# The first norm's row factor moved behind the projection, and the first weight unit in two halves

## The reference, cut to what matters

```
x: (256 tokens, 1024)
h = x * rsqrt(mean(x*x, per token) + 1e-6) * norm1_g
t = h @ w_in                                # 1792 + 1048 + 2048 columns
aq, ak, bq, bks, bkw | av, bvs, bvw, bkc, bvc, bgate | mgate = columns of t
kc, vc = MLP over windows of bkc, bvc;  ya, yb = two kinds of attention
g = sigmoid(mgate + b_merge)                # (256, 2, 1024)
x = x + (g[:,0] * (ya @ w_up_a) + g[:,1] * (yb @ w_up_b)) @ w_out
x = x + peer_ffn(...)                       # then cross-attention, FFNs
```

## Time and profile before

| | us |
|---|---|
| runs shown: median (lowest, highest) | 1786.71 (1786.55, 1787.03) |
| the profiled execution | 1786.81 |
| its span, from the first to the last instruction | 1785.0 |
| TensorE busy | 1750.7 |
| VectorE, ScalarE, GpSimd busy | 1204.4, 1001.4, 489.2 |

### The profile page before, as it was taken

One profiled execution on the slowest core, in us unless ns is written; L12 is line 12 of the kernel. 1 busy time (PEld: TensorE's weight loads), 2 busy tenths in 40 slices (PEclk: granted clock), 3 DMA queues, 4 the chain that ended last, 5 costly groups with the idle time before them and its releaser, 6 DMA issues.

```text
span 1785.0 us, 30696 instructions
## 1 busy us (share of the span) xinstructions
PE 1750.7 (98%) x10764; PEld 1545.4 (87%) x10764; DVE 1204.4 (67%) x2466; ACT 1001.4 (56%) x1679; POOL 489.2 (27%) x245
## 2 busy tenths in 40 slices
PE   8998999999999999999999999999999999999998
PEld 7895899899878888888888888877999988989997
DVE  6757849899765555555555555876579965669974
ACT  5567565469445555555555555666565545556553
POOL 0150166379144444444444444000000000000000
PEclk9999999999999999999999999999999999999999
DMA  7560454601455555555556665634455564545552
GB/s 292 200 236 13 150 193 152 226 25 48 165 194 193 189 189 191 192 191 188 188 190 237 239 216 177 241 142 166 145 192 189 189 199 144 177 131 177 189 196 76
DMA packets 84719, 313.70 MB, mean 176 GB/s; under 512 B 9360, under 2 KB 9488, under 8 KB 83216
## 3 DMA queue, kind: packets, MB, share of 16 engines
q1 hardware_dynamic: 82912, 304.44, 50.8%
q10 hardware_dynamic: 1712, 7.97, 1.2%
HBM read 304.77 MB, written 7.60 MB: 175 GB/s over the span
## 4 chain that ended last, share of the span: by engine, by line
PE 85%; issue 6%; DVE 4%; ACT 3%; POOL 2%; PEld 1%; DMA 0%; DVEq 0%; POOLq 0%; ACTq 0%; PEldq 0%
PE bank L798 80%; PE bank L1249 3%; POOL wsplit L1400 1%; ACT projq L1579 1%; ACT probs L1579 0%; POOL wsplit L1431 0%; PEld bank L1249 0%; PE bank L843 0%; PE bank L832 0%; DVE wsplit L1891 0%; DVE projq L2106 0%; DVE att L2092 0%; DVE attn L2089 0%; PE bank L1070 0%; DVE probs L2104 0%
## 5 line engine op out<-in xcount | busy, mean ns | idle before, releaser
L798 PE MATMUL bank<-HT,wsplit 128*128 128x256 f32 (+1 forms) x5056 | 720.3, 301 | 1.6 <-DVE HT L1934 0.9
L798 PEld LDWEIGHTS bank<-HT,wsplit 128*128 128x128 f32 x5056 | 679.1, 189 | 47.4 <-issue 3.7
L1431 POOL TENSOR_TENSOR wsplit<-raw,wsplit 128x1024 fp32r<-128x1024 f32 x111 | 278.0, 2505 | 380.1 <-ACT wsplit L1757 380.1
L798 PE MATMUL bank<-wsplit,wexp 128*128 128x512 f32 x1536 | 371.0, 392 | 0.6 <-DVE wexp L2372 0.6
L1757 ACT ACTIVATE wsplit<-raw 128x1024 fp32r<-128x1024 f32 x238 | 240.2, 1053 | 181.0 <-PE bank L798 180.6
L798 PEld LDWEIGHTS bank<-wsplit,wexp 128*128 128x128 f32 x1536 | 280.2, 188 | 57.1 <-DVE wsplit L2347 2.1
L2347 DVE TENSOR_TENSOR wsplit<-raw,wsplit 128x1024 fp32r<-128x1024 f32 x127 | 156.9, 1236 | 103.8 <-ACT wsplit L1757 103.6
L1466 ACT ACTIVATE wsplit<-raw 128x1024 fp32r<-128x1024 f32 x148 | 156.4, 1059 | 111.6 <-PE bank L798 110.5
L1891 DVE TENSOR_TENSOR wsplit<-raw,wsplit 128x1024 fp32r<-128x1024 f32 x124 | 154.5, 1258 | 78.5 <-ACT wsplit L1466 77.6
L1891 DVE TENSOR_TENSOR wsplit<-raw1b,wsplit 128x1024 fp32r<-128x1024 f32 x102 | 122.5, 1221 | 44.0 <-ACT wsplit L1466 43.6
L1466 ACT ACTIVATE wsplit<-raw1b 128x1024 fp32r<-128x1024 f32 x102 | 107.5, 1058 | 76.3 <-PE bank L798 72.0
(11 more groups left out here) (288 smaller groups left out, 2070.2 us busy)
## 6 DMA issues: line engine op xcount, KB each, us to landing
raw<-weights SPq DMA_DIRECT2D x148, 512.0 KB, 4.2
raw<-expert_v SPq DMA_DIRECT2D x127, 512.0 KB, 3.8
raw<-expert_u SPq DMA_DIRECT2D x119, 512.0 KB, 4.3
raw1b<-weights SPq DMA_DIRECT2D x102, 512.0 KB, 4.3
raw1a<-weights SPq DMA_DIRECT2D x48, 512.0 KB, 4.5
early_u<-expert_u SPq DMA_DIRECT2D x5, 512.0 KB, 3.7
raw1a<-expert_u SPq DMA_DIRECT2D x4, 512.0 KB, 4.3
parked<-memT SPq DMA_DIRECT2D x1, 2048.0 KB, 7.3
```

The costliest lines, as they stand in the source:

```text
L798: ins = pe.matmul(out, lhsT, rhs, start=start, stop=stop, **kw)
L1431: pool.tensor_tensor(wsplit[:, s, 1, :], raw0[:, s, :], f32(wsplit[:, s, 0, :]), ALU.subtract).then_inc(u_lo, 1)
```

## The change

TensorE transposes X unscaled, the first group of columns as soon as each token block has landed, with no filling before and five filling products behind. The squares, roots and reciprocals come later on ScalarE and VectorE. Where the projection has tokens on the partitions, its copies out of the banks multiply by the factor. For the merge gates the factors have to run along the free dimension: VectorE spreads each block's factors over 128 columns of `act_e`, TensorE transposes them behind the projection, ScalarE copies the result into `row_of_tokens`. VectorE multiplies a gate's bank by that row into `mgate` and frees the bank; ScalarE's sigmoid then works in `mgate`. Gate 7's copy becomes such a product on VectorE. The first weight unit is loaded, rounded and split in two halves, and TensorE begins with its first.

```diff
@@ -101,11 +101,11 @@ def bank_groups()
-    out += [(("mg", 0), "a")] + [(("win2", kv), "d") for kv in range(2)]
-    out += [(("mg", g), "a") for g in range(1, 4)]
-    out += [(("hid", kv), "d") for kv in range(2)] + [(("mg", 4), "a")]
+    out += [(("mg", 0), "d")] + [(("win2", kv), "d") for kv in range(2)]
+    out += [(("mg", g), "d") for g in range(1, 4)]
+    out += [(("hid", kv), "d") for kv in range(2)] + [(("mg", 4), "d")]
...
@@ -329,6 +329,7 @@
+        row_of_tokens, row_factors = act_e[:, 0, :], act_e[:, 1, :]
@@ -675,7 +678,9 @@ SyncE
-            for u in range(4):
+            sp.dma_start(raw0[:, 0, 0:512], weights[0][:, 0:512]).then_inc(first_landed, 16)
+            sp.dma_start(raw0[:, 0, 512:1024], weights[0][:, 512:1024]).then_inc(w_landed[0], 16)
+            for u in range(1, 4):
                 load(u, u)
@@ -879,12 +884,27 @@ TensorE
+            def first_unit(banks, src, fresh):
+                for k in range(2):
+                    if k == 0:
+                        pe.wait_ge(first_lo, 1)
+                        w = lambda part: wsplit[:, 0, part, :].rearrange("p (k n) -> p k n", k=2)
+                    else:
+                        w = tiles_of(weights_of("win", 0, 0), k=2)
+                    wait_turned(fresh, k)
+                    for t in range(T):
+                        mm3(banks[t][:, :], lambda a: src[:, a, k, tok(t)], lambda b: w(b)[:, k, :], k == 0, False)
...
@@ -1092,9 +1112,25 @@ TensorE
+            def turn_as_landed(X, landed, b, fill):
+                for n in range(4):
+                    for t in range(T):
+                        if n == 0:
+                            pe.wait_ge(landed[t], 16)
+                        for k in range(2):
+                            c = 2 * n + k
+                            ins = pe.transpose(PS[n][:, (k * T + t) * P:(k * T + t + 1) * P], X[:, t, c * P:(c + 1) * P], ident)
+                    ins.then_inc(norm_t, 1)
+                keep_busy(b, fill)
+
             pe.wait_ge(in_small, 16)
-            turn("norm1", H1, PS[7], (5, 2, 0))
+            turn_as_landed(X1, in_x, PS[7], 5)
             token_major("win", N_WIN, HT, "norm1", PROJ - 512 * (N_WIN - 1))
+            pe.wait_ge(row_made, T)
+            for t in range(T):
+                ins = pe.transpose(PS[0][:, tok(t)], row_factors[:, tok(t)], ident)
+            ins.then_inc(row_full, 1)
@@ -1515,12 +1552,22 @@ ScalarE, norm_out
-                    if (name, b) == ("norm1", 2):
-                        split_to(3)
...
+                    if (name, b) == ("norm1", 0):
+                        first_unit()
+                    if name == "norm1" and b in (1, 2):
+                        split_to(b + 1)
+
+            def first_unit():
+                act.wait_ge(first_landed, 16)
+                act.activation(wsplit[:, 0, 0, 0:512], raw0[:, 0, 0:512], ACT.Copy).then_inc(first_hi, 1)
+                act.wait_ge(w_landed[0], 16)
+                act.activation(wsplit[:, 0, 0, 512:1024], raw0[:, 0, 512:1024], ACT.Copy).then_inc(w_hi, 1)
+                split[0] = 1
@@ -1579,10 +1626,6 @@ ScalarE, attention_by_pairs
-                    if (use, step) == ("ab", 1):
-                        act.wait_ge(last_gate_full, 1)
-                        act.activation(mgate[:, 6:8, 1, :], bank(("mg", 7))[:, :].rearrange("p (c n) -> p c n", c=2),
-                                       ACT.Copy).then_inc(last_gate_out, 1)
@@ -1610,30 +1653,33 @@ ScalarE
+            act.activation(root_table, eps, ACT.Sqrt)
+            norm_out("norm1", HT)
             norm_sums("norm1", X1, H1, lambda t: act.wait_ge(in_x[t], 16))
-            split_to(2)
-            norm_out("norm1", HT)
             for n in range(N_WIN):
                 full(("win", n, 1))
...
-                    ins = act.activation(dst, bank(("win", n, 1))[:, cols], ACT.Copy)
+                    ins = act.activation(dst, bank(("win", n, 1))[:, cols], ACT.Copy, scale=stat[:, 5:6])
...
             wait_freed(act, ("win", N_WIN - 1, 0))
             wait_freed(act, ("win", N_WIN - 1, 1))
+            act.wait_ge(row_full, 1)
+            act.activation(row_of_tokens, PS[0][:, 0:S], ACT.Copy).then_inc(row_out, 1)
             act.activation(gate3, projv[:, :, BG - NORMED:PROJ - NORMED], ACT.Sigmoid).then_inc(gate3_done, 1)
...
             def merge_gates(gs):
                 for g in gs:
-                    full(("mg", g))
-                    for c in range(2):
-                        n = 2 * g + c
-                        ins = act.activation(mgate[:, n % KD, n // KD, :], bank(("mg", g))[:, c * S:(c + 1) * S],
-                                             ACT.Sigmoid, bias=smalls[:, BMERGE][:, n:n + 1])
-                    ins.then_inc(bank_freed["a"], 1)
+                    split_to(units_to(("mg", g)) + 3)
+                    wait_freed(act, ("mg", g))
+                    for n in (2 * g, 2 * g + 1):
+                        act.activation(mgate[:, n % KD, n // KD, :], mgate[:, n % KD, n // KD, :], ACT.Sigmoid,
+                                       bias=smalls[:, BMERGE][:, n:n + 1])
@@ -2128,22 +2189,38 @@ VectorE
                     if (use, step) == ("ab", 1):
+                        dve.wait_ge(last_gate_full, 1)
+                        dve.tensor_tensor(mgate[:, 6:8, 1, :], bank(("mg", 7))[:, :].rearrange("p (c n) -> p c n", c=2),
+                                          row_of_tokens.unsqueeze(1).to_broadcast([P, 2, S]), ALU.mult).then_inc(last_gate_out, 1)
                         compressed_softmax()
...
-            norm_scale("norm1", X1, H1)
             norm_out("norm1", HT)
+            split_to(3)
+            row_scales("norm1")
+            for t in range(T):
+                dve.tensor_copy(row_factors[:, tok(t)], stat[:, 4 + t:5 + t].to_broadcast([P, P])).then_inc(row_made, 1)
...
-                    ins = dve.tensor_copy(dst, bank(("win", n, 0))[:, cols])
+                    ins = dve.tensor_scalar(dst, bank(("win", n, 0))[:, cols], stat[:, 4:5], None, ALU.mult)
...
+            def scale_gates(gs):
+                for g in gs:
+                    full(("mg", g))
+                    dve.tensor_tensor(mgate[:, 2 * g % KD:2 * g % KD + 2, g // 4, :],
+                                      bank(("mg", g))[:, :].rearrange("p (c n) -> p c n", c=2),
+                                      row_of_tokens.unsqueeze(1).to_broadcast([P, 2, S]), ALU.mult).then_inc(bank_freed["d"], 1)
+
+            dve.wait_ge(row_out, 1)
+            scale_gates([0])
             dve.wait_ge(in_layer1, 16)
...
+            scale_gates(range(1, 4))
...
-            split_to(units_to(("mg", 4)) + 3)
+            scale_gates([4])
...
-            split_to(units_to(("mg", 5)) + 3)
+            scale_gates([5])
...
-            split_to(units_to(("mg", 6)) + 3)
+            scale_gates([6])
```

29 lines of the change are left out of this document (25 added, 4 removed).

## The result

The changed kernel takes 1795.92 us (median of 6 runs, 1794.98 to 1797.31) against 1786.87 (median of 6, 1786.55 to 1787.16): ratio 1.0051, 95% interval 1.0041 to 1.0061. It is slower by 9.05 us. I had forecast 1792.6, with 1788.6 to 1794.8 as the range: the sign was right, the size was too small by 3.3 us, and the time lies above the range. The profiled execution took 1797.19, the second longest of the six, with a span of 1795.5; its time is 10.4 more than that of the one of before (1786.81).

A forecast was written before the change was run, and what follows sets the result against it. TensorE, busy 98% of the span, was taken to bound the kernel. 1786.81 - 1.5 (start) + 6.7 (3.4 first gates, 3.3 last gates) + 0.65 (attention) = 1792.6 us, range 1788.6 to 1794.8.

The forecast's parts named there:

- the sign: Whole kernel: the change makes it slower; slower by over 0.2% (above 1790.3 us) was given a chance of 0.70.
- First gates, +3.4: First four merge gates: the late start is not won back, so TensorE takes unit 35 at 105.9, a loss of 3.4 us.
- The loop of 6.0: Merge gates: sigmoids, rounded copies, low parts and product form a serial ring of 6.0 us against TensorE's 5.87 per gate.
- The rule of the Trainium skill: Low parts: a two-SBUF-input VectorE instruction and a GpSimd instruction reading SBUF exclude each other; the first holds its whole length.
- the loop of 4.7: Merge gates: the loop's length in us if VectorE and GpSimd did not exclude each other; the lag would shrink 1.2 a gate.
- Last three gates, +3.3: Gates 4 to 6 and head transposes: 2.0 waited for gate 6's product, another wait behind, kcT at 139.7; 3.3 us more loss.
- Attention, +0.65: Attention: gate 7's product on VectorE ahead of the compressed softmax loses 0.65 us, bounds 0.2 and 0.75.
- rival d: Start: gains nothing, as TensorE idles and its clock rises only after the projection began; with the lag 1794.2 us; chance 0.07.
- The start, -1.5: Start: first projection matmul at 11.05 instead of 12.54, set by the filling products, a gain of 1.5 us.
- (a): First four gates: the lag is absorbed, leaving 0.7 at unit 35 and 3.1 in the last gates; 1789.8 us; chance 0.20.
- (b): Whole kernel: not slower, TensorE the only bound and only its start counts; needs a shorter loop; 1785.3 us; chance 0.12.

The follow-up runs named there:

- The order experiments: The changed kernel with ScalarE's gate sigmoids put later, 1785.78 us, and the changed kernel with VectorE's product ahead of its low part, 1788.46 us.
- e4_product_first: The changed kernel, but VectorE forms each gate's product before its low part of the next even unit: 1788.46 us, ratio 1.0007.
- filled waits: The changed kernel with products into an unused bank in TensorE's waits ahead of the fourth and fifth pair of head transposes: 1793.55 us, ratio 1.0039.
- e8_table_early: The changed kernel with the attention gates' sigmoid and its table load ahead of ScalarE's wait for the row: 1793.93 us, ratio 1.0040.
- f2_before_gate7_vector: The kernel before with one edit, gate 7's bank copied by VectorE instead of ScalarE: 1787.65 us, ratio 1.0004.
- e2: The changed kernel's gates (row, products, gate 7 on VectorE) with the start of the kernel before: 1795.51 us, ratio 1.0049.
- e3_sigmoids_later: The changed kernel with each gate's sigmoids behind ScalarE's part of the next units' splitting, all products kept: 1785.78 us, ratio 0.9994.
- f1_gate7_scalar: The changed kernel with sigmoids later, plus gate 7 copied by ScalarE and multiplied by VectorE behind the attention: 1785.72 us, ratio 0.9990.
- f4_best_no_filling: The changed kernel with sigmoids later, gate 7 copied by ScalarE and no filling products ahead of the projection: 1785.65 us, ratio 0.9991.
- h2_best_gates_alone: The kernel before's start with the changed gates, sigmoids later, table early, gate 7 copied by ScalarE and multiplied behind the attention: 1786.70 us, ratio 0.9999.

## Why the prediction was right or wrong

**First gates, +3.4: right.** Measured 3.74. The loop of 6.0 was 6.02, VectorE's low parts under GpSimd's 2.50, 2.58 and 2.55 where one alone takes 1.22, the product 0.68 to 0.69, the table load behind the row's copy. The order experiments took the ring apart and the loss went. The wait split into 0.96 at unit 33 and 3.03 at unit 35, where I had one of 3.4. The rule of the Trainium skill ("SBUF — State Buffer", section "Who interferes with whom") fits these durations; in e4_product_first, where the two copies don't meet in the gates, VectorE's takes 1.22. No run here lets them meet without the exclusion, so the loop of 4.7 was not tried.

**Last three gates, +3.3: right, but short of the clock.** Waits of 2.08 and 1.09 stand where I had 2.0 and one more behind it. Measured 4.63 in the changed kernel, with filled waits 3.39 (kcT 5.60 later, unit 35 2.21 later), and 3.37 in e8_table_early with open waits and no fall. The difference of 1.2 to 1.3 is the half clock of twelve transposes.

**Attention, +0.65: right for the move itself, but a term is missing.** The move itself is worth 0.60 in the filled profile (73.11 for 72.51), the only one with gate 7 on VectorE and no fall in the attention. The changed kernel has 2.84. The other 2.2 us are two falls of the clock, of 7 and 3.5 us. I had priced every added wait at its own length. Some of them were followed by a fall of TensorE's clock, and in f2_before_gate7_vector this move alone was. The trace of before has a number that could have warned me: in the attention of before TensorE is busy 63.33 of 73 us, so idle already, and I added waits to it. This is the step that failed: **no term for the clock once TensorE idles in the middle of the program**, though the text had one for the start (rival d).

**The start, -1.5: right in the profile, not in the medians.** The profile shows 11.35 behind the filling products, 1.19 earlier, with the small inputs 0.30 later than in the old trace; 11.05 was forecast. But one pair of profiles is a thin base: the four kernels with the old start begin the projection at 11.54, 11.88, 12.01 and 12.54, and the seven with the new one and five filling products at 9.80 to 11.35. Their means, 11.99 and 10.72, are 1.3 apart. The start alone moves the median by 0.7, and with the gates as changed by nothing (e2 1795.51, changed 1795.92). The clock's rise is one part: the ten filling passes take 2.18 or 1.28 as it comes late or early. What else takes the gain away in the medians stays open.

**Added up** for the profiled execution: -1.2 + 3.7 + 3.3 + 0.6 = 6.4 by the mechanisms of the prediction and 3.5 by the clock, together 9.9 of the 10.3 at the out-projection; 0.3 lie between kcT and the first scores, 145.86 - 140.20 against 138.38 - 133.02, the end of the fall at 141. The profiled execution is 1.3 above the median, so the clock's share of the median's 9.05 is smaller (an estimate: 9.05 - 6.4 = 2.7); the two executions with the highest mean clock, 0.998, are the fastest of the six (1794.98 and 1795.10). With the waits filled, 1793.55 lies inside the range.

**Rivals.** (a), the lag absorbed, is what e4_product_first became once VectorE's order was turned, not the changed kernel. (b), TensorE the only bound at 1785.3, is e3_sigmoids_later (1785.78): it needed a shorter ring, as said. (d), 1794.2 from a start that gains nothing, was nearest in number, and the medians bear out half of it; but it puts the loss at the start, and the two extra microseconds are in the attention.

Open: in f1_gate7_scalar and f4_best_no_filling the executions fall into two groups some 1.5 us apart. Part follows the mean clock, but four of f4's ten took 1785.6 to 1785.8 with a mean clock of 1.0, and h2_best_gates_alone has two such at 1787.35 and 1787.79, so a second cause is left that no profile caught. Open too is what decides whether a wait brings a fall: the wait of 2.77 in e8_table_early did, the one of 3.03 in the changed kernel didn't.

## What to carry to other kernels

When a step moves from one engine to another, draw the ring: which engine now waits, what is queued behind that wait, and whether the one it waits for needs that queued work. A ring as long as the bound engine's own pace never wins back a delay, though every engine is half idle, and putting the waiting instruction behind the work that others need broke it here at no cost that could be measured. Price a new wait of TensorE twice where it already idles: its own length, and a chance of half-speed work behind it. Here one fall of some 3.3 us made the attention 0.6 to 1.3 us longer in seven profiles. That is less than half its length, and one reason shows in the rows: TensorE is busy without a gap in it (3.40 of 3.40 us in f2_before_gate7_vector), so it also takes the place of waits.
